# First loads moved ahead of two attentions, clearing moved to ScalarE, and small work moved to the sample part

## The chip, the cores and the metric

One core of a Trainium2 chip runs the whole program. Its engines are TensorE (PE, with its weight loads as PEld), VectorE (DVE), ScalarE (ACT), GpSimd (POOL) and SyncE (SP, which only issues DMAs here). The metric is the device time of one execution, in microseconds, lower is better.

## What is computed

The reference is one inference step of a streaming encoder with two layers, on 1024 prompt tokens and 32 sample tokens of width 1024 (float32). What touches the change:

```
layer 0: z = h @ w_in                       # one projection for both mixers
  A (8 heads): score = sum_h w_h * relu(qi_h . ki);  keep the 256 best keys of each query
     logits = q.k / 8 + t5_bias[k_pos - q_pos];  p = softmax(logits);  o = p @ v
  B (4 heads): f = lb + (1 - lb) * sigmoid(fb)       # lb = softmax of lb_logits
     S_t = diag(f_t) S_(t-1) + (1 - f_t) v_t^T ;  o_t = S_t^T silu(q_t)
     o = rmsnorm(o) * g_norm * silu(gate)
  x += gate1 * ([A, B] @ w_out);  x += gate2 * swiglu(modulate(rmsnorm(x)))
layer 1: the same with C (16 heads): attention over a band of 9 chunks of 64 tokens,
  logits = q.k / 8 + rel_bias[clip(q_pos - k_pos)]
y = rmsnorm(x)
```

The 32 sample tokens have their own caches of keys and values (2048 past keys in A, 512 in C). They are worked on after the prompt in each attention: this is the sample part.

## The kernel before

The program is a sequence of stages, each built in a `Tools` block: `front_phase` (line 1525: norms, adaLN factors, the projection of layer 0, the scores and the choice of 256 keys), `attention_phase` for A (named `pa`, line 2068), `recurrence` for B (line 2723), `trunk_phase` 0 (line 298: output projection, FFN, and the projection of layer 1), `attention_phase` for C (named `pc`), and `trunk_phase` 1. `Tools.block` puts a barrier of all engines ahead of each stage (line 79). In a stage each engine runs its own list of instructions in order, and semaphores order them against each other. A transfer is issued by SyncE (`sp.dma_start`) or ScalarE (`act.dma_start`) and counts up a semaphore by 16 when it has landed.

**The attentions.** Heads go in pairs, 4 in A and 8 in C, and each pair has 8 tiles of 128 queries. A tile of a pair is a unit `u`. For each unit TensorE makes the scores of both heads (line 2284) into `dots`. VectorE adds the bias and finds the least value (`tensor_tensor_reduce`, line 2420, shown as CUSTOM_DVE_ANT_0 followed by a read of the accumulator). ScalarE takes the exponential (line 2523), TensorE turns the result (line 2297), VectorE and ScalarE copy it out in turn (lines 2429 and 2532), and TensorE multiplies with the values (line 2312). TensorE's order is scores of `s`, turns of `s - 2`, values of `s - 3`. In A the bias and the mask of the chosen keys have to be added first, which GpSimd does into `extra` (line 2255); in unit 16 it adds the sample masks, too (line 2239). In C, GpSimd only writes two corners of each pair's bias (lines 2249 and 2250).

The loads of a pair are `q`, `k`, `bias` and `v`, in two buffers each. SyncE issues those of pairs 0 and 1 at the start of the stage in this order, then the sample's, then the weights or the recurrence's first inputs, and then those of pair `g + 2` as pair `g` is done. `skew_a` and `skew_c` in DRAM hold the biases; the front stage writes them.

The sample part follows after the last unit: per group of four heads scores (line 2342), logits (line 2457), exponential (line 2543), turns (line 2353), copies (lines 2471 and 2555), values (line 2373), and a scaling by the reciprocal of the sum (lines 2478 and 2483).

**Small work inside A.** `RecurrenceHead` makes what the recurrence needs first: the bounds `lb` of f in `bound_differences` (two VectorE operations, lines 2646 and 2648), `bound_exponentials` (ScalarE, line 2653) and `bounds` (four VectorE operations, lines 2658 to 2664), and in `gains` the factors of the three later norms (six VectorE operations, lines 2684 and 2687). All are on tiles of 4 to 16 columns. They are placed among the units of A, at `s = 16`, `18` and `20` of 32.

**The recurrence.** It runs in three rounds of 384 tokens. In each, GpSimd makes `k = 1 - f` (line 2869), and then per level it multiplies `k` (line 2883) while VectorE multiplies `r` (line 2895) and selects out of TensorE's `ring` into `near` (line 2904). TensorE's matmuls of pairs (lines 3113 to 3121) wait for both. `near`, `att`, the first state and the padding of f, q and v must be cleared or set to one beforehand. GpSimd does that in `clear`, in round 0 between the complements and level 0 (lines 2851 to 2863). ScalarE turns f and q of rounds 1 and 2 into decays and SiLUs meanwhile (lines 2998, 3001, 2993), and then copies out of the `ring` into `att` (line 3024).

Of the kernel before, what the change touches and what calls it, by code (L numbers as in the profile page):

```python
# [6 lines left out]

# [7 lines left out]
F32 = mybir.dt.float32  # L15
# [282 lines left out]
def trunk_phase(nc, io, l, x, c, places, early):  # L298
# [11 lines left out]
    with Tools(nc) as m:  # L310
# [68 lines left out]
        y_stored = m.sem(f"{name}_y_stored")  # L379
        block = m.block()  # L380
# [106 lines left out]
        def _(sp):  # L487
# [1037 lines left out]
def front_phase(nc, io, moving, low_at, score, c):  # L1525
# [6 lines left out]
    with Tools(nc) as m:  # L1532
        raw = [m.sb(f"f_raw{b}", [P, 2 * KD * P]) for b in range(2)]
# [35 lines left out]
        choose, store_mask = choosing(m, score, io["mask_s"], q)  # L1569
        block = m.block()  # L1570
# [32 lines left out]
        def _(sp):  # L1603
# [52 lines left out]
            for u in range(2, len(units)):  # L1656
# [411 lines left out]
def attention_phase(nc, name, io, z, q0, k0, vt, v0, skew, width, heads, back, mask, side, ident, mix, early=None, next_weights=None):  # L2068
# [36 lines left out]
    with Tools(nc) as m:  # L2105
        q, k = ([m.sb(f"{name}_{x}{b}", [P, T]) for b in range(2)] for x in "qk")
        v = [m.sb(f"{name}_v{b}", [P, TILES, P]) for b in range(2)]
        bias_all = m.sb(f"{name}_bias", [P, 2, 2, width])
        bias = [bias_all[:, b] for b in range(2)]
        extra_all = m.sb(f"{name}_extra", [P, 4, T]) if mask is not None else None  # L2110
        extra = [extra_all[:, a, :] for a in range(4)] if mask is not None else None
        prob_all = m.sb(f"{name}_prob", [P, 6 * max(keys)])
        prob = [prob_all[:, max(keys) * a:max(keys) * a + max(keys)] for a in range(6)]
        probT = [m.sb(f"{name}_probT{a}", [P, 2 * max(keys)]) for a in range(2)]
        least, total, inv = (m.sb(f"{name}_{x}", [P, 2 * U]) for x in ("least", "sum", "inv"))
        spread = [m.sb(f"{name}_spread{b}", [P, 4 * P]) for b in range(2)]
        oT = [m.sb(f"{name}_oT{b}", [P, T]) for b in range(2)]
# [3 lines left out]
        s_q = m.sb(f"{name}_s_q", [P, G, 4, S])  # L2121
        s_k_new, s_v_new = m.sb(f"{name}_s_k_new", [P, 2 * G, S]), m.sb(f"{name}_s_v_new", [S, 256 * G])
        own_sides = G if mask is None else 1
        s_k = [m.sb(f"{name}_s_k{g}", [P, 2, side.past]) for g in range(own_sides)]
        s_v = [m.sb(f"{name}_s_v{g}", [P, side.blocks, 256]) for g in range(own_sides)]
        if mask is not None:
            s_k.append(extra_all[:].rearrange("p (c a) n -> p c (a n)", c=2))
            s_v.append(bias_all[:].rearrange("p b h n -> p (b h n)").rearrange("p (i n) -> p i n", n=256))
        s_bias = [m.sb(f"{name}_s_bias{g}", [P, side.keys]) for g in range(G)]
        s_prob = [] if mask is None else [m.sb(f"{name}_s_prob", [P, side.keys])]  # L2130
        s_prob += [prob_all[:, side.keys * b:side.keys * b + side.keys] for b in range(2 - len(s_prob))]
        s_mask = s_prob[0]
        s_tail = [m.sb(f"{name}_s_tail{b}", [S, P]) for b in range(2)]
        s_least, s_total, s_inv = m.sb(f"{name}_s_least", [P, G, 4]), m.sb(f"{name}_s_sum", [P, G]), m.sb(f"{name}_s_inv", [P, G])
        s_o = [m.sb(f"{name}_s_o{b}", [P, DH]) for b in range(2)]
        s_oT = [m.sb(f"{name}_s_oT{b}", [DH, P]) for b in range(2)]
# [25 lines left out]
        def _(sp):  # L2162
            def loads(g):
# [3 lines left out]
                sp.dma_start(q[b][:], z[q0 + g][:, 0:T]).then_inc(qk_in[b], 16)  # L2167
                sp.dma_start(k[b][:], z[k0 + g][:, 0:T]).then_inc(qk_in[b], 16)
# [1210 lines left out]
```

## Time and profile before

| | |
|---|---|
| runs | 3110.88, 3113.55, 3113.63 us, median 3113.55 |
| profiled execution | 3111.68 us, of which its span is 3109.8 us |
| PE busy | 2917.9 us (94%) |
| DVE busy | 1653.1 us (53%) |
| POOL busy | 1321.6 us (42%) |
| ACT busy | 951.2 us (31%) |
| mean granted clock of TensorE | 0.971 of full speed |

The span is the time from the first to the last instruction in the profile. Its stages, by the first instructions after each barrier: front 0 to 580 us, attention A 580 to 760, recurrence 760 to 885, trunk 0 885 to 2006, attention C 2006 to 2270, trunk 1 2270 to 3110. Busy shares over the whole span are averages over stages that differ; what an edit is worth has to be read in its stage. In a timeline row the number in brackets is the time the engine sat idle ahead of that instruction, with what ended it.

### The profile page before, as it was taken

Reading aid. Unit: us, or ns where it says so; the run is one execution under the profiler, and the core shown is the slowest. Engines: PE = TensorE matmul, PEld = TensorE weight load, DVE = VectorE, ACT = ScalarE, POOL = GpSimd, SP = SyncE. Lnnn points to the kernel's source line nnn. Section 1 sums busy time; section 2 is a strip of 40 time slices with the busy share of each in tenths; the row PEclk is TensorE's granted clock in tenths of the full one; section 3 lists DMA queues with packets and bytes.
Section 4 is the critical chain, followed back from the end, with each engine's and each line's share of the span. In section 5 each row is a group of like instructions: output and inputs, shape, how many; then the busy total and the mean of one; then the engine's idle time right before and its main releaser. Section 6 shows DMA issues by size and latency. Waiting matters only on the chain. (4 is left out here: it accounts for less than half of the span.)

```text
span 3109.8 us, 60214 instructions
## 1 busy us (share of the span) xinstructions
PE 2917.9 (94%) x25097; PEld 2716.4 (87%) x25097; DVE 1653.1 (53%) x2959; ACT 951.2 (31%) x1984; POOL 1321.6 (42%) x1082
## 2 busy tenths in 40 slices
PE   7999999886789899999999999899889999999998
PEld 5859999664679899999999999766689999999998
DVE  6399999564646644445346400055536644444345
ACT  3341211354433433332101311165524333332001
POOL 2112212373533877776334222100114877775334
PEclk8999999998889999999999999999989999999999
DMA  5816763633241122223321232352121122224222
GB/s 211 256 61 228 235 212 106 180 108 110 99 164 55 49 83 83 82 70 133 102 83 62 81 103 74 95 191 86 64 85 45 66 83 80 71 78 153 83 74 72
DMA packets 160465, 338.82 MB, mean 109 GB/s; under 512 B 21033, under 2 KB 94529, under 8 KB 152193
## 3 DMA queue, kind: packets, MB, share of 16 engines
q1 hardware_dynamic: 119856, 281.64, 27.0%
q10 hardware_dynamic: 40336, 53.31, 4.8%
q8 instruction: 200, 3.28, 0.4%
q14 instruction: 73, 0.59, 0.1%
HBM read 268.30 MB, written 79.49 MB: 112 GB/s over the span
## 5 line engine op out<-in xcount | busy, mean ns | idle before, releaser
L108 PE MATMUL tr_acc<-tr_quad_hi,ah_ring_hi 128*128 128x264 f32 x2432 | 696.3, 286 | 18.8 <-DVE tr_kept L1142 13.2
L110 PE MATMUL tr_acc<-tr_quad_hi,ah_ring_lo 128*128 128x264 f32 x2432 | 694.7, 286 | 0.0
L109 PE MATMUL tr_acc<-tr_quad_lo,ah_ring_hi 128*128 128x264 f32 x2432 | 692.4, 285 | 0.0
L552 POOL TENSOR_TENSOR ah_ring_lo<-ah_raw,ah_ring_hi 128x512 fp32r<-128x512 f32 (+1 forms) x402 | 553.9, 1383 | 183.0 <-ACT ah_ring_hi L889 169.2
L108 PEld LDWEIGHTS tr_acc<-tr_quad_hi,ah_ring_hi 128*128 128x128 f32 x2432 | 461.0, 190 | 19.7 <-DVE tr_kept L1142 13.6
L109 PEld LDWEIGHTS tr_acc<-tr_quad_lo,ah_ring_hi 128*128 128x128 f32 x2432 | 461.2, 190 | 0.1
L110 PEld LDWEIGHTS tr_acc<-tr_quad_hi,ah_ring_lo 128*128 128x128 f32 x2432 | 460.4, 189 | 0.0
L550 POOL CAST ah_ring_hi<-ah_raw 128x512 fp32r<-128x512 f32 (+1 forms) x172 | 113.4, 659 | 592.3 <-PE tr_acc L110 527.2
L108 PE MATMUL tr_acc<-tr_part_hi,ah_ring_hi 128*128 128x352 f32 x1038 | 335.5, 323 | 2.0 <-DVE tr_kept L1191 2.0
L109 PE MATMUL tr_acc<-tr_part_lo,ah_ring_hi 128*128 128x352 f32 x1038 | 332.8, 321 | 0.0
L110 PE MATMUL tr_acc<-tr_part_hi,ah_ring_lo 128*128 128x352 f32 x1038 | 332.5, 320 | 0.0
L1228 DVE SCALAR_TENSOR_TENSOR x<-tr_acc,mod,x 128x352 f32<-128x352 f32 (+2 forms) x384 | 166.8, 487 | 265.6 <-PE tr_acc L110 265.6
L2420 DVE CUSTOM_DVE_ANT_0 pc_prob<-pc_dots,pc_bias 128x640 f32<-128x640 f32 (+4 forms) x128 | 83.2, 652 | 348.0 <-POOL pc_bias L2250 268.2
L1412 DVE TENSOR_SCALAR_CACHE_REDUCE f_q<-score,choose_trial 128x384 bf16<-128x384 f32 (+6 forms) x224 | 242.1, 1146 | 1.1
L889 ACT ACTIVATE ah_ring_hi<-ah_raw 128x512 fp32r<-128x512 f32 x230 | 143.5, 626 | 248.1 <-POOL ah_raw L567 177.5
L108 PE MATMUL f_acc<-h_hi,f_w_hi 128*128 128x352 f32 x600 | 202.3, 337 | 6.8 <-DVE h_lo L2016 6.8
L108 PEld LDWEIGHTS tr_acc<-tr_part_hi,ah_ring_hi 128*128 128x128 f32 x1038 | 194.8, 188 | 2.5 <-DVE tr_kept L1191 2.4
L109 PEld LDWEIGHTS tr_acc<-tr_part_lo,ah_ring_hi 128*128 128x128 f32 x1038 | 195.0, 188 | 0.1
L110 PEld LDWEIGHTS tr_acc<-tr_part_hi,ah_ring_lo 128*128 128x128 f32 x1038 | 194.6, 187 | 0.0
L1714 POOL CAST f_w_hi<-f_raw 128x2048 fp32r<-128x2048 f32 (+1 forms) x15 | 28.4, 1895 | 389.9 <-DMA f_raw<-in_w_dram 197.4
L110 PE MATMUL f_acc<-h_hi,f_w_lo 128*128 128x352 f32 x600 | 193.6, 323 | 0.0
L109 PE MATMUL f_acc<-h_lo,f_w_hi 128*128 128x352 f32 x600 | 193.5, 322 | 0.0
(399 smaller groups left out, 6484.6 us busy)
## 6 DMA issues: line engine op xcount, KB each, us to landing
f_ada_w<-in_w_ada_dram SPq DMA_DIRECT2D x48, 1024.0 KB, 5.5
scratch_inner<-tr_kept ACTq DMA_DIRECT2D x88, 264.0 KB, 2.4
tr_staged<-scratch_inner SPq DMA_DIRECT2D x44, 528.0 KB, 4.0
ah_raw<-in_w_gate_dram SPq DMA_DIRECT2D x44, 512.0 KB, 3.5
ah_raw<-in_w_up_dram SPq DMA_DIRECT2D x44, 512.0 KB, 4.5
ah_raw<-in_w_down_dram SPq DMA_DIRECT2D x64, 256.0 KB, 3.1
f_raw<-in_w_dram SPq DMA_DIRECT2D x24, 512.0 KB, 7.4
out_z_dram<-f_stage ACTq DMA_DIRECT2D x60, 176.0 KB, 1.9
```

Of the source, the lines that this page charges most:

```text
L108: pe.matmul(out, w_hi, hi, start=start, stop=False)
L109: pe.matmul(out, w_hi, lo, start=False, stop=False)
L110: return pe.matmul(out, w_lo, hi, start=False, stop=stop)
L550: pool.tensor_copy(hi[:, 0:width], own).then_inc(w_hi, 1)
L552: pool.tensor_tensor(lo[:, 0:width], own, hi[:, 0:width].bitcast(F32), ALU.subtract).then_inc(w_ready, 1)
L889: act.activation(slot(u, to)[0], factor_of(u, to), ACT.Copy).then_inc(act_hi, 1)
L1228: done = dve.scalar_tensor_tensor(out=x[:, k, lo:hi], in0=pair[s % 3][:, a, lo - THIRD * t:hi - THIRD * t], scalar=gate_ffn[:, k, of:of + ...
L1412: last = dve.tensor_scalar(marks[n % 2][0:p, 0:width], score[0:p, at:at + width], bound(p, j), 0.0, compare, ALU.add, accum_out=count[0:p, ...
L1714: pool.tensor_copy(w[b].hi[:, 0:n], raw[b][:, 0:n]).then_inc(w_hi, 1)
L2420: dve.tensor_tensor_reduce(prob[2 * (u % 3) + hd][:, 0:n], dots[hd][:, at_dots(u):at_dots(u) + n], add, -DH ** -0.5, 3.0e38, ALU.add, ALU. ...
```

## The change

There are three edits.

1. **First pair loaded early.** A new class `FirstPair` holds `bias`, `q` and `k` of pair 0 of an attention, at a fixed place. In A it is the place of the front's `f_raw` buffers. In C it lies in the trunk's arena from `11 * QUAD` on. The three loads are issued by SyncE in the stage before: in the front after its last weight load, when the bias lines are out, the last weights are split and all outputs but those of the last two units are stored, and in trunk 0 after its last weight load, when the outputs of the first five units of the projection are stored. SyncE waits for them at the end of that stage. The attention then issues only `v` for pair 0, and GpSimd and TensorE no longer wait for bias, `q` and `k` of pair 0. The attention's other tiles are laid around the place that is kept.
2. **Clearing by ScalarE.** `clear` leaves GpSimd. ScalarE fills `near` and `att` at the start of the recurrence (a copy of `c.ones`, broadcast, times the value), and the first state and the paddings after the decays of round 1.
3. **Bounds and gains in the sample part.** `bound_differences` goes behind the last unit and ahead of the first sample logits, `bound_exponentials` behind the last sample exponential, `bounds` and `gains` between the copies and the scaling of the last sample group.

The diff, cut to its core:

```diff
+class FirstPair:
+    def __init__(self, m, name, z, q0, k0, skew, width, at):
+        nc = m.nc
+        self.at, self.end = at, at + 8 * width + 8 * T
...
+        self.sources = (z[q0][:, 0:T], z[k0][:, 0:T], shifted(skew[0:2], P, width + P - 1, P - 1, width))
+        self.landed = m.sem(f"{name}_first")
+
+    def loads(self, sp):
+        q, k, bias = self.sources
+        sp.dma_start(self.bias[:], bias).then_inc(self.landed, 16)
+        sp.dma_start(self.q[:], q).then_inc(self.landed, 16)
+        sp.dma_start(self.k[:], k).then_inc(self.landed, 16)
+
+    def done(self, sp):
+        sp.wait_ge(self.landed, 48)
... trunk_phase, SyncE, behind the last weights
+            if ahead:
+                for r in range(3):
+                    sp.wait_ge(stored[r], 16 * 2 * 5)
+                ahead.loads(sp)
+                ahead.done(sp)
... front_phase, SyncE, behind the last weights
+            sp.wait_ge(lines_out, 48)
+            sp.wait_ge(w_ready, len(units))
+            projected = store_no[plan.last_step[len(units) - 3]] + 1
+            for r in range(3):
+                sp.wait_ge(stored[r], 16 * len(range(r, projected, 3)))
+            ahead.loads(sp)
             store_mask(sp)
-            sp.wait_ge(lines_out, 48)
+            ahead.done(sp)
... attention_phase, SyncE
-                sp.dma_start(q[b][:], z[q0 + g][:, 0:T]).then_inc(qk_in[b], 16)
-                sp.dma_start(k[b][:], z[k0 + g][:, 0:T]).then_inc(qk_in[b], 16)
+                if g:
+                    sp.dma_start(q[b][:], z[q0 + g][:, 0:T]).then_inc(qk_in[b], 16)
+                    sp.dma_start(k[b][:], z[k0 + g][:, 0:T]).then_inc(qk_in[b], 16)
... the same for bias; GpSimd and TensorE
-                if i == 0:
-                    pool.wait_ge(bias_in[b], 16 * (g // 2 + 1))
+                if i == 0 and g:
+                    pool.wait_ge(bias_in[b], 16 * ((g + 1) // 2))
-                if i == 0:
-                    pe.wait_ge(qk_in[b], 32 * (g // 2 + 1))
+                if i == 0 and g:
+                    pe.wait_ge(qk_in[b], 32 * ((g + 1) // 2))
... VectorE, among and behind the units
-                if head and s == U // 2:
-                    head.bound_differences(dve)
-                elif head and s == U // 2 + 4:
-                    head.bounds(dve)
-                    head.gains(dve)
+            if head:
+                head.bound_differences(dve)
             for s in range(G + 1):
                 if s < G:
                     side_logits(s)
...
+                    if head and s == G:
+                        head.bounds(dve)
+                        head.gains(dve)
                     side_scale(s - 1)
... ScalarE
-                if head and s == U // 2 + 2:
-                    head.bound_exponentials(act)
             for s in range(G + 2):
                 if s < G:
                     side_exp(s)
+                if head and s == G - 1:
+                    head.bound_exponentials(act)
... recurrence, GpSimd
-                if n == 0:
-                    clear()
... recurrence, ScalarE
+            def fill(tile, value):
+                shape = tile.shape
+                source = c.ones[0:shape[0], 0:shape[2]].unsqueeze(1).to_broadcast(list(shape))
+                return act.activation(tile, source, ACT.Copy, scale=value)
+
+            for b in range(2):
+                fill(near[b][:], 0.0).then_inc(near_zero, 1)
+            for b in range(2):
+                fill(att[b][:], 0.0).then_inc(att_zero, 1)
+
+            def clear():
+                fill(state[0][:], 0.0).then_inc(state_zero, 1)
+                fill(f[ROUNDS - 1][:, :, N - ROUND * (ROUNDS - 1):], 1.0).then_inc(f_pad, 1)
+                fill(q[ROUNDS - 1][:, :, N - ROUND * (ROUNDS - 1):], 0.0).then_inc(q_pad, 1)
+                for rows in (slice(32, 64), slice(64, P)):
+                    fill(v[rows, TILES, :].rearrange("p (a n) -> p a n", a=HB), 0.0).then_inc(v_pad, 1)
... behind the decays of round n
+                if n == 1:
+                    clear()
```

## Rows read from the trace of the kernel before

**Rows 1.** Windows: stretch, length, busy us (instructions) by engine, PEclk, DMA share, GB/s.
```profile
1000.00:1900.00 900.00, 886.44 (x6377) 883.09 (x6376) 387.55 (x538) 227.21 (x399) 493.11 (x412) 0.99 0.24 83
...
2006.00:2014.00 8.00, 1.66 (x8) 0.93 (x8) 0.33 (x3) 1.28 (x1) 1.01 (x4) 0.50 0.88 286
...
2270.00:3110.00 840.00, 814.93 (x6140) 813.02 (x6140) 414.64 (x599) 227.03 (x402) 475.18 (x389) 0.98 0.24 82
```

**Rows 2.** Timeline, head of A: start, us, engine, line, operation, count, idle before.
```profile
579.96 0.46 POOL L2232 MEMSET pa_s_q<- 64x128 f32 x2 [46.55 <-POOLq L79]
587.74 22.73 POOL L2255 TENSOR_TENSOR pa_extra<-pa_bias,score 128x128 f32<-128x128 f32 x18 [7.32 <-DMA pa_bias<-scratch_skew_a]
...
594.35 0.70 PE L2312 MATMUL pa_out<-pa_probT,pa_v 128*64 128x128 f32 x4
```

**Rows 3.** DMA of the first v in A; landings of all pa_v, then pc_v loads.
```profile
pa_v<-out_zt_dram SPq DMA_DIRECT2D x1, 512.0 KB, 8.0
...
DMA to landing us min/median/max: 3.9/8.3/13.5
...
DMA to landing us min/median/max: 3.9/5.0/10.6
```

**Rows 4.** Timeline, head of C.
```profile
2006.15 0.67 POOL L2232 MEMSET pc_s_q<- 64x256 f32 x2 [49.10 <-POOLq L79]
2013.07 0.20 POOL L2249 MEMSET pc_bias<- 64x128 f32 x1 [6.25 <-DMA pc_bias<-scratch_skew_c]
...
2019.04 0.44 PE L2312 MATMUL pc_out<-pc_probT,pc_v 128*64 128x128 f32 x4
```

**Rows 5.** Timeline, A: longest logits of pairs two to four, small work of pair three.
```profile
643.49 1.23 DVE L2420 CUSTOM_DVE_ANT_0 pa_prob<-pa_dots,pa_extra 128x1024 f32<-128x1024 f32 x1 [2.44 <-PE pa_dots L2284]
...
659.94 0.20 ACT L2653 ACTIVATE hg_lbt<-hg_lb 128x8 f32<-128x8 f32 x1
...
665.22 1.14 DVE L2658 TENSOR_TENSOR hg_lbt<-hg_lbt 128x4 f32<-128x4 f32 x1
...
669.14 0.95 DVE L2420 CUSTOM_DVE_ANT_0 pa_prob<-pa_dots,pa_extra 128x768 f32<-128x768 f32 x1
...
678.72 1.23 DVE L2420 CUSTOM_DVE_ANT_0 pa_prob<-pa_dots,pa_extra 128x1024 f32<-128x1024 f32 x1 [2.44 <-PE pa_dots L2284]
...
711.78 1.23 DVE L2420 CUSTOM_DVE_ANT_0 pa_prob<-pa_dots,pa_extra 128x1024 f32<-128x1024 f32 x1 [2.44 <-PE pa_dots L2284]
```

**Rows 6.** Timeline, sample part of A.
```profile
728.33 1.23 DVE L2457 CUSTOM_DVE_ANT_0 pa_s_prob<-pa_dots,pa_s_bias 128x1024 f32<-128x1024 f32 x1 [0.62 <-PE pa_dots L2342]
...
738.58 0.58 ACT L2555 ACTIVATE pa_probT<-pa_turn 128x512 f32<-128x512 f32 x1
...
749.02 0.15 DVE L2478 RECIPROCAL pa_s_inv<-pa_s_sum 128x1 f32<-128x1 f32 x1
753.99 0.28 DVE L2483 TENSOR_SCALAR pa_s_o<-pa_out,pa_s_inv 128x64 f32<-128x64 f32 x1 [4.81 <-PE pa_out L2373]
```

**Rows 7.** Timeline, recurrence, round 0 and the start of round 1.
```profile
759.90 2.33 POOL L2869 TENSOR_SCALAR hg_k<-hg_f 128x768 f32<-128x768 f32 x2 [51.64 <-POOLq L79]
...
764.40 0.56 DVE L2895 TENSOR_TENSOR hg_r<-hg_r,hg_f 128x384 f32<-128x384 f32 x1 [0.49 <-PE hg_ring L3113]
...
765.32 1.49 ACT L2998 ACTIVATE hg_f<-hg_f 128x1536 f32<-128x1536 f32 x1 [9.27 <-DMA hg_f<-out_z_dram]
...
768.01 2.31 POOL L2883 TENSOR_TENSOR hg_k<-hg_k,hg_f 128x384 f32<-128x384 f32 x2
...
778.08 1.17 ACT L2993 ACTIVATE hg_q<-hg_q 128x1152 f32<-128x1152 f32 x1 [2.55 <-DMA hg_q<-out_z_dram]
...
783.24 0.67 ACT L3024 ACTIVATE hg_att<-hg_ring 32x192 f32<-32x192 f32 x2 [4.00 <-PE hg_ring L3118]
...
786.48 0.38 PE L3118 MATMUL hg_ring<-hg_r,hg_k 128*32 128x32 f32 x6 [2.36 <-issue]
...
795.72 1.55 POOL L2883 TENSOR_TENSOR hg_k<-hg_k,hg_f 128x384 f32<-128x384 f32 x1 [1.68 <-PE hg_ring L3113]
```

More of the change, by code:

```diff
@@ L8 @@
+import math
 from contextlib import ExitStack
@@ L295, in done, with trunk_phase @@
         pool.wait_ge(self.w_lo, AHEAD)
-def trunk_phase(nc, io, l, x, c, places, early):
+def trunk_phase(nc, io, l, x, c, places, early, next_pair=None):
     last = l == 1
@@ L379, in trunk_phase @@
         y_stored = m.sem(f"{name}_y_stored")
+        ahead = next_pair(m, base + 11 * QUAD) if next_pair else None
+        assert ahead is None or ahead.end <= base + 14 * QUAD
         block = m.block()
@@ L1569, in front_phase @@
         choose, store_mask = choosing(m, score, io["mask_s"], q)
+        ahead = next_pair(m, raw_at)
+        assert ahead.end <= raw_at + 2 * 8 * KD * P
         block = m.block()
@@ L2065, in __init__, with attention_phase @@
         self.quads = [(lo, min(lo + 4, self.blocks)) for lo in range(0, self.blocks, 4)]
-def attention_phase(nc, name, io, z, q0, k0, vt, v0, skew, width, heads, back, mask, side, ident, mix, early=None, next_weights=None):
+class FirstPair:
+    def __init__(self, m, name, z, q0, k0, skew, width, at):
+        nc = m.nc
+        self.at, self.end = at, at + 8 * width + 8 * T
+        self.bias = nc.alloc_sbuf_tensor_at(f"{name}_bias0", [P, 2, width], F32, offset=at)
+        self.q, self.k = (nc.alloc_sbuf_tensor_at(f"{name}_{x}0", [P, T], F32, offset=at + 8 * width + 4 * T * n)
+                          for n, x in enumerate("qk"))
+        self.sources = (z[q0][:, 0:T], z[k0][:, 0:T], shifted(skew[0:2], P, width + P - 1, P - 1, width))
[7 more added lines that the diff above has]
+        sp.wait_ge(self.landed, 48)
+def attention_phase(nc, name, io, z, q0, k0, vt, v0, skew, width, heads, back, mask, side, ident, mix, first, early=None, next_weights=None):
     pairs = heads // 2
@@ L2105, in attention_phase, with sb @@
     with Tools(nc) as m:
[L2106 to L2110, printed above, removed]
+        def sb(tile, shape):
+            if nc.sbuf_base <= first.at < nc.sbuf_base + 4 * math.prod(shape[1:]):
+                m.sb(f"{name}_kept_free", [P, (first.end - nc.sbuf_base) // 4])
+            return m.sb(tile, shape)
+        q, k = [first.q, sb(f"{name}_q1", [P, T])], [first.k, sb(f"{name}_k1", [P, T])]
+        v = [sb(f"{name}_v{b}", [P, TILES, P]) for b in range(2)]
+        bias = [first.bias, sb(f"{name}_bias1", [P, 2, width])]
+        extra_all = sb(f"{name}_extra", [P, 4, T]) if mask is not None else None
         extra = [extra_all[:, a, :] for a in range(4)] if mask is not None else None
-        prob_all = m.sb(f"{name}_prob", [P, 6 * max(keys)])
+        prob_all = sb(f"{name}_prob", [P, 6 * max(keys)])
         prob = [prob_all[:, max(keys) * a:max(keys) * a + max(keys)] for a in range(6)]
[L2114 to L2117, printed above, removed]
+        spread = [sb(f"{name}_spread{b}", [P, 4 * P]) for b in range(2)]
+        probT = [sb(f"{name}_probT{a}", [P, 2 * max(keys)]) for a in range(2)]
+        least, total, inv = (sb(f"{name}_{x}", [P, 2 * U]) for x in ("least", "sum", "inv"))
+        oT = [sb(f"{name}_oT{b}", [P, T]) for b in range(2)]
         dots = [m.ps(f"{name}_dots{a}", [P, 1024]) for a in range(2)]
```

56 lines of the change are left out of this document (26 added, 30 removed).

## The prediction

> **What bounds the kernel now.** I read first the table of windows, then the timelines of each engine at the places that the diff names, and last the grouped pages of the tiles involved. The windows say where an improvement can count at all. In the two trunk stretches TensorE is busy 886 of 900 us and 815 of 840 us, and nothing in the diff touches them. In the first 8 us of the second attention it is busy 1.66 us, while the DMA share is 0.88 [rows 1]: a wait for first loads, and the first attention begins in the same way. The stages run one after another with a barrier of all engines between them (line 79), so what a stage loses at its head, the end loses too, unless something later in that stage has a date of its own.
>
> **Head of the first attention.** After the barrier GpSimd clears the sample queries in 0.46 us and then has nothing until the bias of the first pair lands, at 587.74, an idle 7.32 us; from there its additions run without a gap, 18 of them in 22.73 us, so GpSimd paces the whole first pair [rows 2]. With bias, q and k already there, the additions begin at 579.96 + 0.46 = 580.4: 7.3 us earlier. What is late next? The values of this pair are not loaded early. Before, that load was queued behind q, k and bias and landed 8.0 us after its issue; the shortest landing of one of its four loads was 3.9, the longest 13.5 [rows 3]. Now it is issued first, at 579.96. Its first reader ran at 594.35 [rows 2] and will run 7.3 earlier, at 587.1. With 3.9 the load lands at 583.9 and costs nothing; with 8.0 at 588.0, costing 0.9; with 13.5 at 593.5, costing 6.4. I take nothing, since 3.9 belongs to a load with an empty queue before it, and keep 0.9 to 7.3 as the gain here.
>
> **Head of the second attention.** The same, with GpSimd's two small mask writes in place of the additions. They waited 6.25 us for the bias, until 2013.07 [rows 4]. Now they start when the clearing of 0.67 us is over, at 2006.82: gain 6.2. The first product with the values was at 2019.04, and moves to 2012.8; the load lands at 2006.15 + 3.9 = 2010.1, and with this stage's longest landing, 10.6 [rows 3], at 2016.8, costing 4.0. So 2.2 to 6.2, and I take 6.2. TensorE is granted half its clock (1.2 GHz) when this stage begins (0.50) [rows 1], and no longer has its first scores done ahead of the bias; this could cost some tenths, and is in the range.
>
> **The early loads themselves.** Each is three more DMA issues on SyncE, in the front behind its last weight load, the split of the last weights and stored outputs, ahead of the store of the sample mask; in the trunk behind all weight loads. Only DMA traffic of the projections' last steps is beside them. GpSimd's last split of weights, which they follow in the front, lies 46.55 us before the attention, and in the trunk 49.10 [rows 2, 4]; the slowest landing in rows 3 is 13.5 us, so they cost nothing. The later pairs' loads are issued with two megabytes less ahead of them.
>
> **Middle of the first attention.** The starts of the longest logits of the second, third and fourth pair are 643.49, 678.72 and 711.78: the third pair, which holds the twelve small operations and the exponential of the bounds, took 35.23 us, the fourth 33.06 [rows 5]. The difference, 2.2 us, goes. It is the stretch from 665.22 to 669.14, in which VectorE ran ten small operations while TensorE had its scores done [rows 5]. The two first ones (bound differences) I leave at nothing, as GpSimd's additions of the sample masks hold up the same step.
>
> **Where that work lands.** The two differences go ahead of the first sample logits, where VectorE has 0.62 us idle [rows 6]. In the middle one of the small operations took 1.14 us beside a working GpSimd [rows 5]; a reciprocal of one column in the sample part, where GpSimd has nothing to do, took 0.15 [rows 6]. I take nothing, at most 0.7. The exponential of 0.20 us [rows 5] goes between the second sample exponential and ScalarE's copy at 738.58, for which TensorE waits [rows 6]: a cost of 0.2. The ten others go ahead of the reciprocal at 749.02, behind which VectorE idles 4.81 us until 753.99 [rows 6]; even at the 3.9 us of the middle they fit. Net 2.0 for the move, bounds 1.3 to 2.4.
>
> **Clearing in the recurrence.** GpSimd cleared between the complements, which ended at 762.2, and its first products with k at 768.01; for those the next pairs of matmuls wait. VectorE's own product of that level, released by the same matmuls, ran at 764.40 [rows 7]. So GpSimd can start at 764.4, 3.6 earlier. But its products then run beside VectorE's: 1.55 us in the next round against 2.31 for two here [rows 7], so the second ends 0.8 later than it would alone. Gain 2.8 to 3.6, taken as 3.1. The GPSIMD Engine Reference of the Trainium skill (Specifications) says that GpSimd's SBUF interfaces are shared with VectorE and contend when that has two SBUF inputs; by this the gain is the 2.8, and without it 3.6. On ScalarE, the four clearings before its first sigmoid are two of 384 and two of 1536 columns. An activation of 1536 columns took 1.49 us, and the first sigmoid waited for its load until 765.32 [rows 7]: about 4.2 us of work from the stage's start at 759.9 on, done at 764.1, free. The five others (about 2.8 us) go behind the first decays. There ScalarE waited 2.55 us for the load of its last SiLU, and 4.00 us for its copy at 783.24 [rows 7]. The first idle takes 2.55 of the 2.8; the copy moves up by 3.1 and leaves 0.9 of the second for the rest. It fits, barely, and costs up to 1.
>
> **Sum.** 7.3 + 6.2 + 2.0 + 3.1 = 18.6 us against the profiled execution's 3111.7: 3093.1. The median of the runs shown is 3113.55, 1.9 above that execution; I put the forecast between, at 3094.0. Worst bounds give 0.9 + 2.2 + 1.3 + 1.8 = 6.2, best ones 7.3 + 6.2 + 2.4 + 3.6 = 19.5, and the places at which the half clock comes and goes shift by a microsecond or two per stage, which is why I allow a few more on either side.
>
> **Rivals.**
> *Round 0 gives nothing back.* In it TensorE stood 2.36 us before 786.48 with nothing to wait for [rows 7]. I read this as instructions that had not arrived. If the wait for k only hid such a wait, the 3.1 us come back as idle time of that kind: 3111.7 - 15.5 = 3096.2. Against it: such a gap should follow TensorE's own progress, and so move with it. The Trainium skill, Runtime: NRT & Kernel Launch (Instruction fetch mechanics), says such fetches are mostly hidden by the rate of issue. By that rule this rival is void; the gap, if it is one, speaks against the rule here.
> *The values are late.* Both value loads land as late as the longest of their kind: 6.4 + 4.0 us lost, gain 8.2, time 3103.5. Against it: by the code the later landings belong to loads queued behind at least 2 MB of others, and these two are queued behind none.
> *The early loads do not do what they say.* Were they issued only when the projection's last outputs are stored, the barrier would wait for them as the attention does now, and only 5.1 us would be won: 3106.6. The code waits for earlier stores only, so this is unlikely.
> *Slower.* The trunks run at a granted clock of 0.99 and 0.98 over 1,740 us [rows 1]. One point less, from pauses that now fall differently, would cost 17.4 us; it decides from 1.07 points (18.6 us), and 1.5 points give 26.1 - 18.6 = 7.5 us more than now, 3119.2. Nothing in the diff alters the trunks' matmuls.
>
> **How the numbers follow.** Forecast 0.67; round 0 gives nothing 0.12; late values 0.10; useless early loads 0.06; slower 0.05. The first three are faster by over 6.2 us (0.2%, about what a measurement here can tell from no change): 0.89. The fourth is within: 0.06. Slower: 0.05. The range of 3087 to 3104 takes in the forecast's bounds, round 0 and late values.
>
> **What would show it.** Right: GpSimd's first addition 0.5 us after the barrier, no wait of TensorE at the first product with the values, GpSimd's mask writes of the second attention 0.7 us after its barrier; pairs three and four of the first attention equally long; the first product with k at the time of VectorE's; no idle time of TensorE behind ScalarE in round 0; trunks equally long. Wrong: idle time put down to the load of v, new gaps without a releaser in round 0, a later copy of ScalarE there, a lower granted clock in the trunks.

## The result and the profile after

The changed kernel takes 3089.32 us (median of four runs, 3086.03 to 3090.57) against 3113.59 of the kernel before beside it. The ratio is 0.9914, 95% interval 0.9897 to 0.9931: 26.8 us less. In a later repeat it was 0.9925 (0.9912 to 0.9937), 23.4 us less. The forecast was 3094.0 with a range from 3087. The median of the four runs lies in that range; by the first ratio the time is 3086.8, just below it. The sign was right and the two heads came out as forecast, but the gain as a whole was under-stated by 5 to 8 us of some 25.

The profiled execution took 3086.03 us. The first lines of its page:

```profile
span 3084.2 us, 60216 instructions
...
PE 2911.6 (94%) x25097; PEld 2711.3 (88%) x25097; DVE 1653.0 (54%) x2959; ACT 956.0 (31%) x1993; POOL 1314.9 (43%) x1073
```

TensorE lost 6.3 us of busy time (2917.9 before) while it does the same matmuls, at a mean granted clock of 0.976 instead of 0.971. In the repeat below it lost 1.6 us, so most of the 6.3 belongs to this one trace. Lengths of the stages, from the first instruction behind one barrier to that behind the next, in us; the third and fourth columns are medians over the traces of all kernels below in which the stage was untouched by the experiment:

| stage | profiled, before | profiled, after | usual without its edits | usual with them | forecast |
|---|---|---|---|---|---|
| front | 579.96 | 579.01 | 580.8 | 580.3 | 0 |
| attention A | 179.96 | 169.61 | 181.0 | 169.9 | -9.3 |
| recurrence | 125.67 | 118.59 | 125.8 | 119.0 | -3.1 |
| trunk 0 | 1120.56 | 1120.21 | 1121 | 1121 | 0 |
| attention C | 263.69 | 256.85 | 263.7 | 257.1 | -6.2 |
| trunk 1 | 839.96 | 839.93 | 839.7 | 840.3 | 0 |

The same stage of the same code differs by up to 3.6 us between traces (the front, 579.5 to 583.1), so single microseconds of the first two columns mean little. By the usual ones A gave 11.1, the recurrence 6.8 and C 6.6, together 24.5.

The heads of both attentions, timeline of GpSimd and of TensorE's first product with the values:

```profile
579.01 0.46 POOL L2280 MEMSET pa_s_q<- 64x128 f32 x2 [46.95 <-POOLq L80]
579.54 22.76 POOL L2303 TENSOR_TENSOR pa_extra<-pa_bias,score 128x128 f32<-128x128 f32 x18
...
586.17 0.70 PE L2360 MATMUL pa_out<-pa_probT,pa_v 128*64 128x128 f32 x4
...
1987.42 0.67 POOL L2280 MEMSET pc_s_q<- 64x256 f32 x2 [48.81 <-POOLq L80]
1988.14 0.20 POOL L2297 MEMSET pc_bias<- 64x128 f32 x1
...
1993.98 0.44 PE L2360 MATMUL pc_out<-pc_probT,pc_v 128*64 128x128 f32 x4
```

These answer to rows 2 and 4. The waits of 7.32 and 6.25 us for the bias are gone, and neither product with the values has an idle time in brackets: they run 7.2 and 6.6 us after the stage's start, and v landed in 4.0 and 4.6:

```profile
pa_v<-out_zt_dram SPq DMA_DIRECT2D x1, 512.0 KB, 4.0
...
pc_v<-out_zt_dram SPq DMA_DIRECT2D x1, 512.0 KB, 4.6
```

The middle and the sample part of A (timeline), where rows 5 and 6 were:

```profile
602.24 1.23 DVE L2468 CUSTOM_DVE_ANT_0 pa_prob<-pa_dots,pa_extra 128x1024 f32<-128x1024 f32 x1 [2.44 <-PE pa_dots L2332]
...
635.30 1.23 DVE L2468 CUSTOM_DVE_ANT_0 pa_prob<-pa_dots,pa_extra 128x1024 f32<-128x1024 f32 x1 [2.44 <-PE pa_dots L2332]
...
717.44 0.17 DVE L2696 TENSOR_TENSOR hg_lb<-hg_lb,hg_lbt 128x8 f32<-128x8 f32 x1
717.96 1.23 DVE L2505 CUSTOM_DVE_ANT_0 pa_s_prob<-pa_dots,pa_s_bias 128x1024 f32<-128x1024 f32 x1 [0.35 <-PE pa_dots L2390]
...
737.91 0.18 DVE L2708 RECIPROCAL hg_lbt<-hg_lbt 128x4 f32<-128x4 f32 x1
...
742.70 0.28 DVE L2531 TENSOR_SCALAR pa_s_o<-pa_out,pa_s_inv 128x64 f32<-128x64 f32 x1 [3.52 <-PE pa_out L2421]
```

Pairs now start 33.06 us apart throughout. VectorE still has 0.35 us idle behind the differences, and 3.52 behind the ten small operations, which together took 1.3 us instead of the 3.9 of the middle.

Round 0 of the recurrence. First TensorE in the kernel before, in the rows that rows 7 do not have:

```profile
775.35 1.17 PE L3113 MATMUL hg_ring<-hg_r,hg_k 128*32 128x32 f32 x67 [1.72 <-issue]
...
780.13 1.39 PE L3113 MATMUL hg_ring<-hg_r,hg_k 128*32 128x32 f32 x84 [0.77 <-issue]
...
786.79 2.96 PE L3121 MATMUL hg_ring<-hg_r,hg_k 128*64 128x64 f32 x24
```

And in the changed kernel: TensorE, GpSimd, ScalarE.

```profile
754.48 0.86 PE L3164 MATMUL hg_ring<-hg_r,hg_k 128*32 128x32 f32 x47 [1.08 <-POOL hg_k L2915]
755.72 1.09 PE L3164 MATMUL hg_ring<-hg_r,hg_k 128*32 128x32 f32 x49 [0.38 <-issue]
...
764.61 1.39 PE L3164 MATMUL hg_ring<-hg_r,hg_k 128*32 128x32 f32 x84 [0.38 <-issue]
...
769.06 2.58 PE L3172 MATMUL hg_ring<-hg_r,hg_k 128*64 128x64 f32 x24 [0.19 <-POOL hg_k L2915]
...
752.88 3.01 POOL L2915 TENSOR_TENSOR hg_k<-hg_k,hg_f 128x384 f32<-128x384 f32 x2 [1.94 <-PE hg_ring L3164]
...
753.59 1.49 ACT L3047 ACTIVATE hg_f<-hg_f 128x1536 f32<-128x1536 f32 x1 [1.33 <-DMA hg_f<-out_z_dram]
...
767.72 0.67 ACT L3075 ACTIVATE hg_att<-hg_ring 32x192 f32<-32x192 f32 x2 [0.20 <-PE hg_ring L3169]
```

GpSimd's first products with k start 4.26 us into the stage, where they started 8.1 in before, and take 1.5 us each beside VectorE. ScalarE's fills leave 1.33 us idle ahead of the first sigmoid and 0.20 ahead of its copy out of the ring: they fit. In this round lies what was not expected, in TensorE's rows. "issue" is idle time for which the profile shows nothing to wait for; before, round 0 held 0.30, 1.72, 0.77 and 2.36 us of it, now it holds 0.38 and 0.38. The last group (64 columns) starts 20.4 us into the stage instead of 26.9.

The trunks, the answer to the first and last of rows 1:

```profile
867.21:1767.21 900.00, 884.00 (x6544) 879.76 (x6545) 450.97 (x659) 248.56 (x449) 492.46 (x408) 0.99 0.25 87
2244.27:3084.20 839.93, 814.18 (x6140) 811.85 (x6140) 416.44 (x600) 226.82 (x402) 475.08 (x389) 0.99 0.24 82
```

### The profile page after: what moved, and what is told of

The parts are those of the page before. It is cut to its first block and busy times, and to the rows that moved or that the text cites. A ratio compares the mean times of both kernels' runs of the same rounds, so it can differ in the third digit from the quotient of the medians.

```text
span 3084.2 us, 60216 instructions
## 1 busy us (share of the span) xinstructions
PE 2911.6 (94%) x25097; PEld 2711.3 (88%) x25097; DVE 1653.0 (54%) x2959; ACT 956.0 (31%) x1993; POOL 1314.9 (43%) x1073
```

## The experiments

The theory after the comparison: the clearing by itself is worth some 3 us as forecast, and the 4 us more come from TensorE's issue gaps, which depend on loads that run at that time. The rivals: the gaps hang on GpSimd's clearing or on TensorE's long wait for it; or the surplus lies elsewhere, or in the chance of one trace.

### One edit at a time

The first kernel is the changed one with edits 2 and 3 undone; the other two are the kernel before with edit 2 or edit 3 made. The diffs are those of the change.

> The kernel before with edit 1 alone, the early first pairs. By the prediction's terms 7.3 + 6.2 = 13.5 us off. If the stretches keep the lengths seen in the changed kernel apart from what edits 2 and 3 touch, the first attention is 7.25 us shorter and the second 6.84. The recurrence must keep its 125.75 us, with the gaps of TensorE of 1.72, 0.77 and 2.36 us: if those shrink here as well, the shift of the head and not the clearing has done it. If the 0.95 us that the front lost came from edit 1, it shows here too and the total is 15.0 us; if it varies by itself, the front lies anywhere between 579.0 and 580.5.

> The kernel before with edit 2 alone, the clearing on ScalarE. Prediction's step: 3.1 us off (bounds 2.8 to 3.6), with TensorE's gaps without a releaser still there, 1.72, 0.77 and 2.36 us, only earlier. Theory now: the gaps shrink with the clearing, since TensorE passes the same places of its program before the 2.1 MB load of the gate, so the recurrence is 6.5 to 7.1 us shorter (118.7 to 119.3 us instead of 125.75). Rival: the gaps depend on the shift of the whole stage or vary from execution to execution, then the recurrence is 3 us shorter, at 122.7.

> The kernel before with edit 3 alone, the small work in the sample part. Prediction's step: 2.2 us off in the third pair of the first attention, 0.2 on in the sample part, 2.0 off in all. The changed kernel's sample part was 0.9 us shorter instead; if edit 3 did that, the attention here is 3.1 us shorter (176.8 instead of 179.88), if not 2.0 (177.9). The recurrence keeps its 125.75 us.

Ratios to the kernel before: edit 1 alone 0.9956 (0.9942 to 0.9969), 13.7 us; edit 2 alone 0.9984 (0.9975 to 0.9992), 5.0 us; edit 3 alone 0.9988 (0.9978 to 0.9999), 3.7 us. The sum is 22.4 and adds up, within the intervals, to the whole. The traces: with edit 1 alone A took 172.77 us and C 259.37. C's head gained what it does in the changed kernel (its sample part starts 233.2 us into the stage, 239.0 before), but the sample part itself was some 2 us longer than in most traces, as it was with edit 3 alone (C 265.17), for which no run shows a cause. The recurrence keeps 124.86 us and its gaps (1.70 and 2.45; the one of 0.77 was 0 there), and the front took 580.84, so its 0.95 us was chance. With edit 2 alone the recurrence takes 117.81 us, 7.9 less, beyond the forecast's 3.1 and beyond the 7.1 of the changed kernel; the runs' ratio bounds it by 2.5 to 7.8 us:

```profile
769.06 0.99 PE L3116 MATMUL hg_ring<-hg_r,hg_k 128*32 128x32 f32 x49 [0.65 <-issue]
...
781.38 0.38 PE L3121 MATMUL hg_ring<-hg_r,hg_k 128*32 128x32 f32 x6 [0.25 <-issue]
781.68 2.96 PE L3124 MATMUL hg_ring<-hg_r,hg_k 128*64 128x64 f32 x24
```

The stage starts at 761.42 here. The gap ahead of the six matmuls is 0.25, where it was 2.36. So the surplus in the recurrence belongs to edit 2 and not to the earlier heads. With edit 3 alone A took 177.35, 2.6 less than the profiled 179.96 but 3.6 less than the usual 181.0. Its sample part was 25.97 us (first sample logits to last scaling), against 25.66 before: the 0.9 us that the changed kernel's sample part was shorter was not edit 3's. In the repeats of that code it took 25.4 to 25.6 us, so the 0.9 was the one trace's.

### Are the gaps due to the gate's load?

(Of the diffs below only the moved load or the added wait is shown; left out are the argument that hands the semaphore over, the removed old load, and the waits that count the parts of a split one.)

Each gap stands at a fixed place of the program: behind matmul 112, 239, 365, 492 and 618 of round 0 in every trace, or nothing shows there. For each such block one packet of 0.02 MB appears on the queue that the profile calls "q8 instruction". The largest gap came while the gate's 2.1 MB landed.

```diff
         sp.dma_start(self.v[:, 0:3, :], v_of[:, 0:3, :]).then_inc(self.v_first_in, 16)
+        sp.wait_ge(pairs_done, 14)
         sp.dma_start(self.gate[:], io["z0"][GB:GB + HB].rearrange("c p n -> p c n")).then_inc(self.gate_in, 16)
```

> The kernel before with one wait more: SyncE issues the gate's load of 2.1 MB in the recurrence only when both matmul groups of level 5 of round 0 are done (about 787 instead of 778.5), so that the last gap of round 0 comes with no such traffic beside it. Theory (TensorE's instructions wait behind the gate's load): the gap of 2.36 us before 786.48 falls to at most 0.5, the one of 1.72 before 775.35, which comes ahead of the gate's load in both, stays. Rival (the gaps come with GpSimd's clearing or with TensorE's long wait for it, and not with traffic): 2.36 stays. Round 1 may be several us longer, since ScalarE needs the gate at its start; the verdict rests on the gap and not on the total.

```profile
779.59 1.18 PE L3114 MATMUL hg_ring<-hg_r,hg_k 128*32 128x32 f32 x67 [1.73 <-issue]
...
790.99 0.37 PE L3119 MATMUL hg_ring<-hg_r,hg_k 128*32 128x32 f32 x6 [2.08 <-issue]
```

A miss: 2.08 us stayed without the gate (recurrence 126.94 us, ratio 0.9996, 0.9986 to 1.0005). Either loads have nothing to do with it, or another load had stepped into the gate's place.

### All loads away, with and without the clearing

The wait stands ahead of the load of q of round 1, so that q, v and gate all come behind round 0. The second kernel has edit 2 on top.

```diff
                 elif landed:
                     sp.wait_ge(landed, 16)
+                    sp.wait_ge(pairs_done, 16)
```

> The kernel before, with the recurrence's loads behind f of rounds 1 and 2 (q, v, gate, v) issued only when round 0's last matmuls are done. Then no load of data runs while TensorE works through the groups after its long wait. New theory, from where the packets of TensorE's instructions start: such a fetch is asked for as TensorE enters the block before, and starts when the data load that is then running has ended. With nothing running it starts within 1.5 us of the entry (3.2 and 3.8 before), and the gaps of 1.72, 0.77 and 2.36 us are at most 0.5 each, GpSimd's clearing and TensorE's wait of about 4.3 us being there as before. Rival (clearing or the long wait makes the gaps): they stay at 1.7 and 2.1 to 2.7. Round 1 is many us longer, as its q comes late; the time of the whole is not the point.

> The kernel above with edit 2 on top, ScalarE's clearing. Both without load traffic behind f in round 0, so what differs is the clearing by itself. From the first product with k to the last group of matmuls of round 0 nothing else changes: the start of the last group (64 columns) comes 2.6 to 3.6 us earlier, counted from the stage's start, than in the one above, against 6.6 us between the kernel before with edit 2 alone and the kernel before. If it is 6 or more here too, the missing 4 us belong to the clearing itself and not to fetches behind loads.

TensorE in the first of them, with GpSimd's clearing (the stage starts at 762.18):

```profile
780.87 1.39 PE L3114 MATMUL hg_ring<-hg_r,hg_k 128*32 128x32 f32 x84 [0.68 <-issue]
...
784.12 0.85 PE L3119 MATMUL hg_ring<-hg_r,hg_k 128*32 128x32 f32 x24 [0.27 <-POOL hg_k L2884]
785.32 2.82 PE L3122 MATMUL hg_ring<-hg_r,hg_k 128*64 128x64 f32 x24 [0.35 <-POOL hg_k L2884]
```

And in the second, with edit 2 (the stage starts at 761.08):

```profile
781.50 2.82 PE L3125 MATMUL hg_ring<-hg_r,hg_k 128*64 128x64 f32 x24 [0.35 <-POOL hg_k L2868]
```

With GpSimd's clearing and TensorE's wait of 4.76 us still there, the gaps of 1.72 and 2.36 are gone; the one of 0.77 stayed at 0.68, a little over what was expected. That excludes the clearing and the long wait as the cause of the two large ones. The last group starts 23.14 us into the stage in the first and 20.42 in the second. So the clearing by itself is worth 2.7 us, and the step from 26.87 to 20.44 in the changed kernel is 2.7 for it and 3.7 for gaps. Both kernels are slower on the whole (1.0026 and 1.0021), since q comes late in round 1.

### Bringing a gap back

The changed kernel, gate's load moved from behind q and v to ahead of f of round 2:

```diff
                 if n > 1:
                     sp.wait_ge(own[0], 16)
+                    if side is self.f:
+                        sp.dma_start(self.gate[:], io["z0"][GB:GB + HB].rearrange("c p n -> p c n")).then_inc(self.gate_in, 16)
```

> The changed kernel with the gate's load of 2.1 MB issued right behind f of round 1 (about 5.5 us into the recurrence) instead of behind q and v. New theory: TensorE enters its third block of instructions 7.1 us into the stage, now at the beginning of a load that runs to about 13; the fetch starts at 11 to 13 instead of 8.25, so the next block is there at 13.6 to 15.6 instead of before 11.3: a gap without a releaser of 2 to 4 us, at the place where the kernel before had its 1.72. The recurrence is 1 to 4 us longer than the 118.6 us of the changed kernel. Rival (no dependence on loads): no gap over 0.5 in round 0. ScalarE's decays of round 2 and the SiLUs come up to 8 us later, which round 1 may feel as well.

```profile
763.33 1.17 PE L3165 MATMUL hg_ring<-hg_r,hg_k 128*32 128x32 f32 x67 [2.11 <-issue]
...
771.96 0.38 PE L3170 MATMUL hg_ring<-hg_r,hg_k 128*32 128x32 f32 x6 [0.84 <-issue]
```

A gap of 2.11 us stands behind matmul 365, where the changed kernel had none, and the recurrence takes 122.37 us instead of 118.6. The total was 0.9932 (0.9912 to 0.9953).

### Which load belongs to which gap

The gate's load in four parts, each behind the landing of the one before; and the first v and the gate both held back, f and q untouched.

```diff
-        sp.dma_start(self.gate[:], io["z0"][GB:GB + HB].rearrange("c p n -> p c n")).then_inc(self.gate_in, 16)
-        sp.wait_ge(self.gate_in, 16)
+        for hd in range(HB):
+            sp.dma_start(self.gate[:, hd, :], io["z0"][GB + hd]).then_inc(self.gate_in, 16)
+            sp.wait_ge(self.gate_in, 16 * (hd + 1))
```

> The kernel before with the gate's load of 2.1 MB as four loads of a head each, every one behind the landing of the one before: the same bytes at the same place, but no long run of one load. Theory (a fetch waits until the load's packets that are already queued have gone): TensorE's fetch, asked for at about 20.2 us into the stage, starts by 22 instead of 23.98, and the gap of 2.36 us (2.08 to 2.70 in four traces) falls to 0.7 or less, while the gap of 1.72 us before it, which belongs to the load of q, stays. Rival (the gap needs only that the DMA engines are busy around it, or hangs on something else at this place): it stays above 1.7. The gate lands several us later, which round 1 may feel.

```diff
         sp.wait_ge(self.q_in[1], 16)
+        sp.wait_ge(pairs_done, 14)
```

> The kernel before with one wait in another place: SyncE issues the first load of v and the gate's load only when both matmul groups of level 5 of round 0 are done. The loads of f and q stay where they were. In the kernel with the gate alone held back the load of v stood right where the gate's had been, and in the one with the gate in pieces v and the first piece together; in both, the packet with TensorE's instructions came as those loads ended. Theory (each gap belongs to the data packets that are queued when TensorE asks): now nothing is queued at the last gap's place, so the gap of 2.36 us (2.45, 2.70, 2.08, 1.62, 1.54 in five others) falls to 0.4 or less, and the gap before, 1.72 us, which belongs to the first load of q, stays at 1.6 to 1.9. Rival (both gaps are of one cause, such as the phase of TensorE against its own long wait, and all the loads had to go for it): both stay, or both shrink.

TensorE at the last gap's place, with the gate in pieces:

```profile
786.42 0.37 PE L3119 MATMUL hg_ring<-hg_r,hg_k 128*32 128x32 f32 x6 [1.62 <-issue]
```

And at both places, with v and the gate held back:

```profile
777.52 1.17 PE L3114 MATMUL hg_ring<-hg_r,hg_k 128*32 128x32 f32 x67 [1.43 <-issue]
...
784.55 0.88 PE L3119 MATMUL hg_ring<-hg_r,hg_k 128*32 128x32 f32 x24 [0.27 <-POOL hg_k L2884]
```

The pieces missed what was expected (0.7 or less): 1.62 stayed. v's first load (768 KB) was issued 0.4 us ahead of the first piece, and both were queued when TensorE entered the block. With both held back, the last gap is gone and the one that belongs to q's load stays, at 1.43 (1.6 to 1.9 was expected). One went, the other stayed: each gap belongs to the loads queued at its own moment. Round 0 was then 3.6 us shorter than before (the first matmul of round 1 at 29.04 us into the stage instead of 32.68), and yet the recurrence took 125.36 and the ratio is 1.0 (0.9989 to 1.0011). Most of it comes back as a gap of the same kind in round 1, behind matmul 995, where the kernel before had none. The loads of v that come behind the gate are issued 4.9 us later than before and are now queued there:

```profile
805.07 0.44 PE L3114 MATMUL hg_ring<-hg_r,hg_k 128*32 128x32 f32 x17 [3.31 <-issue]
```

The packets show the same. DMA view of the kernel before, first 780.2 to 783.6, behind matmul 492 and with the gate's load running, then 783.6 to 785.2:

```profile
DMA packets 495, 1.37 MB, mean 402 GB/s; under 512 B 16, under 2 KB 16, under 8 KB 495
q1 hardware_dynamic: 495, 1.37, 102.0%
...
q1 hardware_dynamic: 152, 0.64, 98.7%
q8 instruction: 1, 0.02, 3.8%
```

And of the kernel without loads, 773.0 to 774.4, behind its matmul 239:

```profile
DMA packets 1, 0.02 MB, mean 12 GB/s; under 512 B 0, under 2 KB 0, under 8 KB 0
...
q8 instruction: 1, 0.02, 4.9%
```

In the kernel before, 495 packets of data and none of instructions pass in the 3.4 us after TensorE entered the block at 780.13; the instruction packet comes in the next window, and the six matmuls of the block after start at 786.48. The packet started at 783.9, 3.8 us behind the entry. Without loads the packet comes at 773.0, 0.9 us behind the entry. In the kernel with the gate held back, q8 has nothing from 784.9 to 788.5, while v's 0.76 MB pass, and one packet right behind.

The same packets say why the changed kernel's gaps are short although the same loads run in it: what counts is how much of the queued load is left when TensorE enters the block. Before, it entered the blocks behind matmul 239 and 492 at 9.94 and 20.21 us into the stage. The first load of q then landed at 13.87 and that of v at 22.65, with the gate's behind it, and the packets started 3.3 and 3.8 us behind the entries. In the changed kernel the entries are at 7.10 and 15.99, the loads that run (f, then q) land at 8.96 and 17.64, and the packets start 1.3 and 1.5 us behind the entries. For the block between them, entered behind matmul 365, the packet did not come sooner (2.2 us instead of 1.7). The gap at its end fell from 0.77 to 0.38 all the same, as TensorE took 0.5 us longer through the block.

### The price of late values, and the clock in the middle of A

The changed kernel with v of pair 0 issued behind the loads of pair 1 (both attentions):

> The changed kernel with the values of pair 0 issued behind the four loads of pair 1 in both attentions, so the margin of the values is gone. In the first attention the load is then behind 1.6 MB or more: landing 8.0 to 13.5 us after the stage's start as in rows 3, first use at 7.16, so TensorE waits 0.9 to 6.4 us for v there and the GpSimd chain (22 us for a pair) takes up some or all of it. In the second the first use comes about 6.6 us after the barrier and nothing is there to take it up: 2 to 4 us lost. Total 2 to 8 us over the changed kernel. If nothing is lost in either, the prediction's rival of late values was void from the start and its bounds too wide.

The waits of TensorE at the head of A (total, times, longest), and then its timeline in C:

```profile
PE pa_out L2362 <- DMA pa_v<-out_zt_dram: 6.2, 1, 6.2
```

```profile
2007.76 0.70 PE L2362 MATMUL pc_out<-pc_probT,pc_v 128*64 128x128 f32 x4 [4.75 <-DMA pc_v<-out_zt_dram]
```

It took 3102.07 us, ratio 0.9964 (0.995 to 0.9978): of the heads' 13.5 us nearly all is lost again (A 176.23, C 262.88; the recurrence took 121.05, 2.5 more than in the changed kernel's trace, of which TensorE's gaps without a releaser in rounds 1 and 2 make 1.6, being 6.3 us in all instead of 4.7; the rest has no cause that a run shows). That is more than the 2 to 8 us expected over the changed kernel: nothing took up the 6.2 us in A. The order of issue of this one load decides edit 1.

In the middle of A, the third pair took 36.8 us in seven traces of kernels with the small operations there, and 35.23 only in the trace that the prediction rests on. TensorE's first scores behind that place, in that trace and then in the one of edit 2 alone:

```profile
671.69 1.77 PE L2284 MATMUL pa_dots<-pa_k,pa_q 64*128 64x512 f32 x8 [2.95 <-DVE pa_least L2420]
```

```profile
671.59 2.68 PE L2284 MATMUL pa_dots<-pa_k,pa_q 64*128 64x512 f32 x8 [2.93 <-DVE pa_least L2420]
```

Stretches (length, busy us by engine, PEclk, DMA share, GB/s) behind it, in the same order:

```profile
671.36:674.76 3.40, 3.07 (x22) 1.88 (x24) 1.52 (x6) 1.70 (x4) 3.40 (x2) 1.00 0.00 0
```

```profile
671.84:675.24 3.40, 3.40 (x13) 1.63 (x12) 0.93 (x1) 0.76 (x2) 2.90 (x2) 0.57 0.00 0
```

Both times TensorE had stood 2.9 us while VectorE ran the ten operations. In one trace it was then granted 1.00 and did 22 matmuls in the stretch, in the other 0.57 (mostly 1.2 GHz) and did 13; the other six traces also show 0.50 there. To test whether the clock makes the difference, the operations were split over three units (sum and reciprocal, then the two others of the bounds, then the gains):

```diff
                 elif head and s == U // 2 + 4:
-                    head.bounds(dve)
-                    head.gains(dve)
+                    head.bounds(dve, 0)
+                elif head and s == U // 2 + 5:
+                    head.bounds(dve, 1)
+                elif head and s == U // 2 + 6:
+                    head.gains(dve)
```

> The kernel before with the ten small operations of bounds and gains in three places (behind units 20, 21 and 22 instead of all behind 20), so that VectorE never holds TensorE for 3.9 us at once. In four of the five traces of kernels with all ten at one place TensorE stood 2.9 us, its granted clock then fell to 0.5 for about 4 us, and the third pair took 36.8 us; in the trace of before the clock stayed at 1.00 and it took 35.23. Theory (1.6 us of it are the clock): with shorter waits the clock stays at 1.00 and the third pair takes 34.0 to 35.3 us. Rival (the operations cost 3.7 wherever they stand, the clock is a bystander): 36.5 or more.

```profile
668.19:671.59 3.40, 2.74 (x18) 1.56 (x18) 3.37 (x4) 2.00 (x5) 3.40 (x2) 1.00 0.00 0
671.59:674.99 3.40, 2.36 (x35) 1.91 (x34) 3.40 (x8) 1.83 (x4) 1.21 (x2) 1.00 0.02 5
```

The clock stays at 1.00 and the third pair takes 34.32 us, as the theory has it, though one of the operations is much dearer than before (2.29 us instead of 0.17, beside GpSimd). On the whole kernel this can't be told from nothing: 0.9999 (0.999 to 1.0008).

### The changed kernel again, and a variant

The variant issues the last v load of the recurrence tile by tile, each behind the landing of the one before, to spare TensorE the gap of 1.74 us that the changed kernel has in round 1.

```diff
-        sp.dma_start(self.v[:, 3:TILES, :], v_of[:, 3:TILES, :]).then_inc(self.v_in, 16)
+        for t in range(3, TILES):
+            sp.dma_start(self.v[:, t:t + 1, :], v_of[:, t:t + 1, :]).then_inc(self.v_in, 16)
+            sp.wait_ge(self.v_in, 16 * (t - 2))
```

> The changed kernel once more, on the same chip as the three below. By the single edits' ratios (13.7, 5.0 and 3.7 us) it is 22 to 27 us faster than the kernel before. Stages as in its first trace, each within the microsecond or two by which the same stage differs between traces: first attention 168.6 to 170.6, recurrence 117.5 to 121, second attention 256 to 258. If the first trace was a lucky one, the gain is nearer to 22 than to 27.

> The changed kernel with the recurrence's last large load (v of tiles 3 to 7, 1.25 MB in one) issued as five loads of a tile each, every one behind the landing of the one before. By the theory of the fetch that waits for the running load, the gap of 1.74 us (1.93 in the kernel with late values) at the 17 matmuls of round 1 falls to 0.9 or less, since the fetch now waits for a load of 0.25 MB. v is not needed before round 2, so the later landing costs nothing. The recurrence gets 0 to 1.5 us shorter; this cannot be told from nothing by the times alone, and the gap decides. If the gap stays at 1.7, the theory does not hold in round 1.

The changed kernel: 3090.07 us, 0.9925 (0.9912 to 0.9937); A 169.97, recurrence 119.51, C 256.99. The variant: 3088.92 us, 0.9924 (0.9911 to 0.9938). In the variant that gap is gone, but in the repeat of the changed kernel it is only 0.26 as well, so the pair says nothing for or against the theory in round 1. (With the late values the same code had 1.93 us there.) No version here beats the changed kernel by more than can be measured.

## Why the prediction was right, and where it failed

**Heads.** Right, mechanism and size. 7.3 and 6.2 were forecast; the first logits moved by 7.24 and 6.2 us, and edit 1 alone gave 13.7 (9.7 to 18.1). The step that the values land in time, by the shortest landing of rows 3, held with 4.0 and 4.6 us. The kernel with v behind other loads showed how much hung on it: 6.2 and 4.75 us of waiting, so that rival's mechanism and its price (10.4) were sound, and its condition did not occur.

**Early loads.** Free, as said. The rival that they are useless falls with that.

**Middle and sample part of A.** The 2.2 us of the one profiled pair were right for that trace, and the work fits where it went (0.35 and 3.52 us idle left). As a price for the median it was mis-sized: 3.7 us is what they cost in seven of eight traces, 1.6 of it at the lower clock after TensorE's wait of 2.9 us. The step was to take a difference between two pairs of a single trace as the usual one. The Trainium skill, TensorE: Matmul & The Clock Gate (Part 1: The HAM clock gate), says that the clock follows how busy TensorE has been of late; the rows agree that it fell behind a wait, and show that the same wait need not bring it down.

**Clearing.** By itself 2.7 us against a forecast of 3.1 (2.8 to 3.6), just under the lower bound, which took GpSimd's products at 1.55 us each beside VectorE; they took 1.5. ScalarE's fills cost nothing, where up to 1 us was allowed.

**The step that failed** is the one on TensorE's gap of 2.36 us: "such a gap should follow TensorE's own progress, and so move with it". It was used only to dismiss the rival in which the gap grows, and never asked whether it could shrink. Its place in the program does move with TensorE; its length does not. Three gaps of 1.72, 0.77 and 2.36 us became 0, 0.38 and 0 (0, 0.12 and 0.52 in the repeat), which up to the last group of matmuls is 3.7 us that no term or bound of the sum held. The runs showed in its place that the length hangs on the loads queued as TensorE enters the block, and a TensorE that is earlier meets other loads. This is the bulk of the miss; the rest is the 1.6 us of clock, and some tenths in C whose cause stays open. Its head does not explain them: up to the sample part C gained 5.8 to 6.3 us (the granted clock in its first 8 us was 0.57 or 0.64, 0.50 before). The rival that round 0 gives nothing back rested on the same reading and was wrong in sign: the gaps gave 3.7 us on top of the clearing's 2.7 and took nothing back.

**Slower.** The trunks kept 0.99 and took the same time within what they vary by.

## What to carry to other kernels

Idle time of TensorE without a releaser is not a constant that can be moved about: read which loads are queued when it appears, and price a shift of TensorE against them in both directions. A difference of 2 us between two stretches of one trace is a sample of one, above all behind a wait of TensorE like the 2.9 us here, behind which the clock dropped in seven traces of eight. And when a first load is moved early, the load that is now first in the queue is what the gain hangs on.

## What the runs showed of the hardware

- TensorE's instructions arrive in blocks of 126 or 127 matmuls of this kind (a weight load and a product each), one packet of 0.02 MB per block; the block's first matmul ran 2.2 to 3.0 us behind the packet's start wherever TensorE stood for it in round 0. Where it stood 1.4 to 2.7 us there, data loads were queued as it entered the block ahead, and the packet started 2.7 to 4.2 us behind the entry. Loads alone do not make such a gap: in the changed kernel, with less of the load left, the packets started 1.3 to 2.2 us behind and the gaps were 0.38 or less (0.52 in the repeat). The Trainium skill, Runtime: NRT & Kernel Launch (Instruction fetch mechanics), calls the cost of such a crossing mostly hidden. For the trunks' long matmuls no trace here contradicts it; for groups of 32 columns, 126 of which are through in some 4 us, it does not hold.
- Even without loads a gap of up to 0.68 us is left at such a place, and the packet started 0.9 to 2.8 us behind the entry. What sets this rest was not tried.
- Three VectorE operations of 4 columns took 1.1 to 2.3 us in some places beside a working GpSimd; the same ones took 0.15 to 0.17 in the sample part, without it. The reciprocal took 0.18 in both.
- After the same wait of 2.9 us TensorE was granted 1.00 in one trace and fell to 0.5 in seven.
